# A two-layer retention and grouped-expert step on one core: states by row group inside the out-projection, squares summed by VectorE, root before reciprocal, logits by chunk with the router weights stationary

## The reference

```python
h = rms_norm(x, g_mix_norm[l]) * (1 + sc1) + sh1
mix, s_new, buf_new = token_mixers(h, ...)     # retention (4 heads of 128) and a 31-tap convolution
x = x + gt1 * (mix @ w_out[l])
h = rms_norm(x, g_ffn_norm[l]) * (1 + sc2) + sh2
ff = grouped_moe(h, w_router, b_router, w_exp_gate[l], w_exp_up[l], w_exp_down[l])
x = x + gt2 * ff
...
# retention, one step of a sampled sequence: the state that is returned
s = s * c_decay + einsum('bjhd,bjhe->bhde', kc * k_decay, vc)
# group norm of a head, and rms_norm: (o - mu) * lax.rsqrt(var + EPS)
# grouped_moe
probs = softmax(h @ w_router + b_router)       # 16 experts in 4 groups
g_sel = argmax(sum of the two best of each group)
wts, local = top_k(cand, 2); wts = wts / sum(wts)
counts = bincount(flat_e, length=16)           # rows of an expert, in blocks
(silu(xb @ w_gate[e]) * (xb @ w_up[e])) @ w_down[e]
```

## Time and profile before

| | before |
|---|---|
| median of 3 runs | 1499.33 us (1494.32 to 1500.7) |
| the profiled execution, its own time | 1502.44 us |
| its span | 1500.3 us |
| TensorE busy | 1428.7 us (95%) |
| VectorE busy | 682.3 us (45%) |
| ScalarE busy | 239.8 us (16%) |
| GpSimd busy | 104.6 us (7%) |
| mean granted TensorE clock | 0.974 |
| moved by DMA | 501.98 MB, 335 GB/s over the span |

### The profile page before, as it was taken

How to read it: one execution, slowest core, us unless ns; L and a number is a source line. 1 busy time by engine, 2 the same in 40 slices (tenths; PEclk the granted TensorE clock), 3 DMA queues, 4 the chain that set the end, 5 groups by cost and what they waited for, 6 DMA issues and landing times.

```text
span 1500.3 us, 19677 instructions
## 1 busy us (share of the span) xinstructions
PE 1428.7 (95%) x6993; PEld 658.7 (44%) x6994; DVE 682.3 (45%) x1986; ACT 239.8 (16%) x392; POOL 104.6 (7%) x149
## 2 busy tenths in 40 slices
PE   6999998999999999999989999999999999999996
PEld 2777664333333233333347766633333333333333
DVE  2697647333323333343338965553333323233333
ACT  1201322111111011111130122211111101111112
POOL 1071111000000000000002511100000000000000
PEclk9899998999999999999999999889999999999998
DMA  9944558999999985899998265589999999979991
GB/s 335 352 175 151 209 204 322 410 409 410 409 410 410 409 321 223 309 410 410 409 409 331 112 242 210 192 330 393 410 410 409 410 409 410 409 299 409 410 410 72
DMA packets 131317, 501.98 MB, mean 335 GB/s; under 512 B 8635, under 2 KB 8955, under 8 KB 131266
## 3 DMA queue, kind: packets, MB, share of 16 engines
q1 hardware_dynamic: 127056, 487.84, 82.5%
q0 software_dynamic: 3600, 11.21, 2.3%
q10 hardware_dynamic: 626, 2.46, 0.6%
HBM read 495.32 MB, written 7.00 MB: 335 GB/s over the span
## 4 chain that ended last, share of the span: by engine, by line
PE 60%; SPq 25%; DMA 5%; DVE 4%; issue 3%; ACT 2%; PEld 1%; PEldq 1%; ACTq 0%; DVEq 0%
PE ps L414 57%; SPq L380 18%; SPq L376 4%; PE ps L417 3%; DMA ring<-in_w_mod 2%; DMA ring<-in_w_exp_up 2%; SPq L396 1%; SPq L318 1%; PEld ps L414 1%; ACT hT L866 1%; ACT arena L866 1%; ACT L866 0%; SPq L382 0%; DVE stat L1053 0%; PEldq L563 0%
## 5 line engine op out<-in xcount | busy, mean ns | idle before, releaser
L414 PE MATMUL ps<-ring,arena 128*64 128x512 f32 x2816 | 635.7, 599 | 16.9 <-DMA ring<-in_w_exp_up 13.8
L414 PEld LDWEIGHTS ps<-ring,arena 128*64 128x64 f32 x2816 | 194.9, 137 | 404.7 <-issue 356.0
L866 ACT ACTIVATE arena<-ps 128x512 f32<-128x512 f32 (+3 forms) x240 | 129.6, 551 | 1124.8 <-PE ps L414 1033.9
L414 PE MATMUL ps<-arena 64*128 64x288 f32 (+4 forms) x1484 | 296.3, 505 | 12.0 <-DVE arena L1383 4.7
L414 PE MATMUL ps<-hT,ring 128*128 128x288 f32 x1024 | 257.9, 414 | 8.4 <-DVE hT L1127 4.1
L1416 DVE SCALAR_TENSOR_TENSOR xT<-ps,mod,xT 128x256 f32<-128x256 f32 x280 | 133.4, 476 | 267.7 <-PE ps L414 267.7
L414 PEld LDWEIGHTS ps<-hT,ring 128*128 128x128 f32 x1024 | 197.8, 194 | 66.4 <-issue 6.9
L414 PEld LDWEIGHTS ps<-arena 64*128 64x128 f32 (+4 forms) x1484 | 119.6, 161 | 203.0 <-issue 180.2
L1158 DVE SCALAR_TENSOR_TENSOR arena<-arena,wcT 128x256 f32<-128x256 f32 x240 | 123.5, 575 | 1.6
L1450 DVE TENSOR_TENSOR arena<-ps,arena 128x512 f32<-128x512 f32 x35 | 24.2, 692 | 195.9 <-PE ps L414 195.9
L417 PE MATMUL ps<-cst,arena 128*128 128x128 f32 (+5 forms) x533 | 83.0, 289 | 12.2 <-DVE arena L1040 7.2
(11 more groups left out here) (173 smaller groups left out, 628.3 us busy)
## 6 DMA issues: line engine op xcount, KB each, us to landing
ring<-in_w_exp_up SPq DMA_DIRECT2D x128, 1024.0 KB, 18.0
ring<-in_w_exp_down SPq DMA_DIRECT2D x128, 1024.0 KB, 17.7
ring<-in_w_exp_gate SPq DMA_DIRECT2D x64, 1024.0 KB, 17.8
ring<-in_w_mod SPq DMA_DIRECT2D x48, 1024.0 KB, 8.9
arena<-in_w_exp_gate SPq DMA_DIRECT2D x32, 1024.0 KB, 17.1
ring<-in_w_in SPq DMA_DIRECT2D x24, 1024.0 KB, 21.4
big<-in_w_exp_gate SPq DMA_DIRECT2D x16, 1024.0 KB, 18.2
hT<-in_w_exp_gate SPq DMA_DIRECT2D x16, 1024.0 KB, 18.4
```

Source lines behind the costliest of these rows:

```text
L414: return nc.tensor.matmul(out, lhsT, rhs, start=start, stop=stop, skip_group_check=True)
L866: return nc.scalar.activation(out, in_, f, **kw)
```

## The change

**Sampled states.** One GpSimd product makes the masked values of all four heads: head h stands in partitions 32h to 32h+31 (`vS` and `kdS` are laid out so by ScalarE copies and VectorE operations). `sample_states(g)` makes half the sequences of all four heads with four matmuls, one per group of 32 rows, each to a bank of its own. It runs inside the out-projection, after blocks 4 and 6, and VectorE adds the states there.

**Second norm.** VectorE adds the squares of chunks 1 to 6 onto that of chunk 0; TensorE sums two chunks instead of eight.

**Root first.** ScalarE takes the root straight from the bank, with the scaling and EPS in the same operation; VectorE takes the reciprocal after it. This holds for the first norm, the layer norm of the convolution, the four heads, the second norm and the last norm.

**Logits.** The router weights are stationary (16 columns), `hT` moves; for each chunk three matmuls write the three token tiles to three column groups. The logits come out expert by token; VectorE copies them, TensorE transposes them to token rows.

**Routing.** Softmax is not normalised; counts come by a matmul of their own, the comparison with block limits and the prefix sum by tables (`thr`, `below`) instead of chains; weights and some clearing are moved to other places.

```diff
+        kdS = kd[:, 2, 0:DH]
+        lgT = stat[:, 0, 0:P]
...
-                def head_states(i):
...
+                def sample_states(g):
+
+                    for h in range(H):
+                        hr = slice(h * NS, (h + 1) * NS)
+                        last = mm(ps[:, STATE_BANK[h], :], kdS[hr, :], vmask[hr, g * 512:(g + 1) * 512], True, True)
                     last.then_inc(V.snew_done, 1)
...
-                pe.wait_ge(V.var_ready, 3)
+                pe.wait_ge(V.rstd_ready, 3)
                 out_block(0, CONV_K)
...
                     out_block(m, RET_K).then_inc(V.outproj_done, 1)
+                    if m == 4:
+                        pe.wait_ge(V.vmask_ready, 1)
+                        pe.wait_ge(V.mod2_added, 3)
+                        sample_states(0)
+                    elif m == 6:
+                        pe.wait_ge(V.snew_ready, 1)
+                        sample_states(1)
...
-                feature_sum(7, sq2, KC, arrived=V.norm2_sq).then_inc(V.norm2_sum, 1)
-                pe.wait_ge(V.mod2_added, 3)
-                head_states(0)
-                head_states(1)
-
-                pe.wait_ge(V.x_mid, KC)
+                pe.wait_ge(V.norm2_acc, 1)
+                mm(ps[:, 7, 0:T], ones, sq2[:, 0, :], True, False)
+                pe.wait_ge(V.norm2_sq, KC)
+                mm(ps[:, 7, 0:T], ones, sq2[:, KC - 1, :], False, True).then_inc(V.norm2_sum, 1)
+                pe.wait_ge(V.x_mid, 7)
                 mod_slab(6, 1, layer_load(2))
                 pe.drain().then_inc(V.mod2_done, 1)
...
+                for k in range(KC):
+                    pe.wait_ge(V.h2_ready, k + 1)
+                    for t, (t0, m) in enumerate(TILES):
+                        last = mm(ps[32 * t:32 * t + E, 4, 0:m], wr[:, k, :], hT[:, k, t0:t0 + m], k == 0, k == KC - 1)
                 last.then_inc(V.logits_done, 1)
...
                         last.then_inc(V.h2_trans, 1)
                         n += 1
-
-                pe.wait_ge(V.h2_copied, 6)
-                head_states(2)
-                head_states(3)
+                        if n == 1:
+                            pe.wait_ge(V.lgT_ready, 1)
+                            tr(ps[:, 5, 0:96], lgT[0:96, :], 96).then_inc(V.lg_trans, 1)
...
-                mm(ps[:, 5, 0:4 * E], ones, mcum[:, :], True, False)
-                last = mm(ps[:, 5, 0:3 * E], C("tri"), rt[:, 10, :], False, True)
-                last.then_inc(V.pos_done, 1)
+                mm(ps[:, 5, 0:3 * E], C("tri"), rt[:, 10, :], True, False)
+                mm(ps[:, 5, E:3 * E], ones, mcum[:, 0:2 * E], False, True).then_inc(V.pos_done, 1)
+                pe.wait_ge(V.m_ready, 2)
+                mm(ps[:, 4, 0:E], ones, rt[:, 12, 0:E], True, True).then_inc(V.cnt_done, 1)
...
-            def root(buf):
-
-                a(buf, buf, ACT.Sqrt).then_inc(V.rstd_ready, 1)
+            def root(buf, bank, n):
+
+                a(buf, ps[:, bank, 0:T], ACT.Sqrt, scale=1.0 / n, bias=C("eps")).then_inc(V.rstd_ready, 1)
...
-                act.wait_ge(V.var_ready, 1)
-                root(stat[:, 1, :])
+                act.wait_ge(x_summed, l + 1)
+                root(stat[:, 1, :], 6, D)
...
+                        for h in range(H):
+                            last = a(vS[h * NS:(h + 1) * NS, :], ps[0:NS, 5, h * P:(h + 1) * P])
+                        last.then_inc(V.v_copied, 1)
...
-            def inverse_var(ch, dst, src, n):
-
-                ch.link(v.tensor_scalar(dst, src, 1.0 / n, EPS, ALU.mult, ALU.add))
-                v.reciprocal(dst, dst).then_inc(V.var_ready, 1)
...
+            def inverse(ch, buf, nth):
+
+                dve.wait_ge(V.rstd_ready, nth)
+                ch.link(v.reciprocal(buf, buf))
...
                 if l == 0:
-                    dve.wait_ge(x_summed, 1)
-                    inverse_var(ch, stat[:, 1, :], ps[:, 6, 0:T], D)
+                    inverse(ch, stat[:, 1, :], 1)
                 dve.wait_ge(slab_step, 4 * l + 2)
                 ch.link(add_turned(2, 1))
...
                 if l > 0:
-                    dve.wait_ge(x_summed, l + 1)
-                    inverse_var(ch, stat[:, 1, :], ps[:, 6, 0:T], D)
-                dve.wait_ge(V.rstd_ready, 1)
+                    inverse(ch, stat[:, 1, :], 1)
...
-                head_var(0)
-                head_var(1)
-                head_mix(0)
-                head_var(2)
-                head_mix(1)
-                head_var(3)
-                head_mix(2)
-                head_mix(3)
+                for h in range(H):
+                    head_mix(h)
...
+                for m in range(4, KC):
+                    add_gated(ch, lambda m: OUT_BANK[m % 4], M_GT1, V.outproj_done, V.x_mid, [m])
+                    if m == 4:
+                        for j in range(1, 4):
+                            ch.link(add_square(j))
+                        add_states(0)
+                    elif m == 6:
+                        ch.link(add_square(4))
+                        ch.link(add_square(5))
+                        add_square(6).then_inc(V.norm2_acc, 1)
+                        add_states(1)
...
+                for t, (t0, m) in enumerate(TILES):
+                    last = v.tensor_copy(lgT[32 * t:32 * t + E, 0:m], ps[32 * t:32 * t + E, 4, 0:m])
+                last.then_inc(V.lgT_ready, 1)
+                dve.wait_ge(V.lg_trans, 1)
...
-                ch.link(v.tensor_reduce(col(2), r3(1), AX.X, ALU.add))
-                ch.link(v.reciprocal(col(2), col(2)))
-                tt(r3(1), r3(1), over_e(col(2)), ALU.mult)
...
+                above = mixed[:, 0:E * (MAXSUB - 1)].rearrange("p (e s) -> p e s", e=E)
+                tt(above, bl(ps[:, 4, 0:E], MAXSUB - 1), C("thr").rearrange("p (e s) -> p e s", e=E), ALU.is_gt)
...
-            v.tensor_scalar(stat[:, 1, :], ps[:, 6, 0:T], 1.0 / D, EPS, ALU.mult, ALU.add).then_inc(fin_rs, 1)
+            dve.sem_inc(tick, 1)
...
-                for i, h in enumerate(STATE_ORDER):
-                    if i >= 2:
-                        pool.wait_ge(V.snew_done, i - 1)
...
-                for i, h in enumerate(STATE_ORDER):
-                    pool.wait_ge(V.snew_ready, i + 1)
-                    pool.dma_start(dstate(rets_v, h), state(h)).then_inc(V.states_stored if i < 2 else V.Sa_stored, 16)
+                gp.tensor_tensor(vmask.rearrange("p (b e) -> p b e", b=B), vS.unsqueeze(1).to_broadcast([P, B, DH]),
+                                 C("smask").unsqueeze(2).to_broadcast([P, B, DH]), ALU.mult).then_inc(V.vmask_ready, 1)
+                pool.wait_ge(V.snew_ready, 2)
+                for h in (2, 3, 0, 1):
+                    pool.dma_start(dstate(rets_v, h), state(h)).then_inc(V.states_stored if h >= 2 else V.Sa_stored, 16)
```

More of the change, by code:

```diff
@@ L68, in constants @@
     c["fold"] = fold.reshape(P, -1)
+    c["eps"] = np.full((P, 1), EPS)
     scale = DH ** -0.5
@@ L952, in _ @@
                 act.wait_ge(V.ln_scaled, 1)
-                act.wait_ge(V.ln_var, 1)
                 for ct in range(CT):
@@ new lines, in _ @@
+                v.tensor_tensor(mcum[:, E:2 * E], M[:, 0:E], M[:, E:2 * E], ALU.add).then_inc(V.m_ready, 1)
+                dve.wait_ge(V.m_ready, 1)
+                v.tensor_tensor(rt[:, 12, 0:E], mcum[:, E:2 * E], M[:, 2 * E:3 * E], ALU.add).then_inc(V.m_ready, 1)
+                pos = ps[:, 5, 0:3 * E].rearrange("p (t e) -> p t e", t=3)
+                dve.wait_ge(V.pos_done, 1)
+                ch.link(v.scalar_tensor_tensor(slot0, pos[:, :, 0], 1000.0, r3(10)[:, :, 0], ALU.add, ALU.mult))
@@ new lines, in _ @@
+                iota = C("iota")
+                for t in range(3):
+                    last = v.tensor_scalar(sel[:, t, :], iota[:, 0:BLK], 1000.0, slot0[:, t:t + 1], ALU.add, ALU.is_equal)
+                last.then_inc(V.sel0_ready, 1)
+                nsubs, starts = rt[:, 14, 0:E], rt[:, 14, E:2 * E]
+                dve.wait_ge(V.cnt_done, 1)
+                above = mixed[:, 0:E * (MAXSUB - 1)].rearrange("p (e s) -> p e s", e=E)
+                tt(above, bl(ps[:, 4, 0:E], MAXSUB - 1), C("thr").rearrange("p (e s) -> p e s", e=E), ALU.is_gt)
@@ new lines, in _ @@
+                ch.link(v.tensor_reduce(nsubs, above, AX.X, ALU.add))
+                v.tensor_scalar(nsubi[:, 0:E], nsubs, 1.0, None, ALU.add)
+                ch.link(v.tensor_scalar(nsubs, nsubs, 1.0, None, ALU.add))
+                ch.link(v.tensor_reduce(rt[:, 14, 2 * E:2 * E + 1], nsubs.unsqueeze(1), AX.X, ALU.add))
+                v.tensor_copy(nsubi[:, E:E + 1], rt[:, 14, 2 * E:2 * E + 1])
+                before = mixed[:, 0:E * E].rearrange("p (e s) -> p e s", e=E)
+                tt(before, bc(nsubs, E), C("below").rearrange("p (e s) -> p e s", e=E), ALU.mult)
@@ new lines, in _ @@
+                ch.link(v.tensor_reduce(starts, before, AX.X, ALU.add))
+                ch.link(v.scalar_tensor_tensor(r3(13), bc(starts, 3), float(BLK), pos, ALU.mult, ALU.add))
+                for k in range(2):
```

(29 more changed lines are left out.)

176 lines of the change are left out of this document (76 added, 100 removed).

## The result

| | before | after |
|---|---|---|
| median, measured side by side | 1496.84 us (4 runs) | 1478.43 us (4 runs, 1476.66 to 1481.89) |
| ratio after/before | | 0.9878 (95% interval 0.9845 to 0.991) |
| the profiled execution; its span | 1502.44; 1500.3 us | 1478.89; 1477.1 us |
| PE / DVE / ACT / POOL busy | 1428.7 / 682.3 / 239.8 / 104.6 us | 1396.5 / 674.9 / 241.5 / 93.1 us |
| mean granted TensorE clock | 0.974 | 0.982 |

What follows compares the result with a forecast made beforehand. Weight loads set the pace, with a chain of waits from last out-projection block to first expert block. Terms 3.2 + 2.0 - 13.45 - 9.65 - 0.5 - 1.7 = -20.1 took 1502.44 to 1482.3, the median to 1479.2; range 1470 to 1491.

Steps and rivals of the forecast that it cites:

- signs that were named: Trace marks for a right forecast, among them second layer's gather about 13 sooner and first odd gate 2.0 after first block.
- First norm: Norm before the in-projection: root first uncovers the reciprocal, +3.2 us in the first layer and +2.0 in the second.
- Heads: First out-projection matmul waits for ScalarE's root instead of VectorE's reciprocal of head 0: -1.1 us in each layer.
- TensorE keeps its clock: Rival: full clock kept in first out-projection matmuls (1.9 us) and gather (2.0), both layers: 7.8 less, 1471.4; chance 0.14.
- States: Sampled states placed inside the out-projection, on four row groups with nearly full overlap: +2.6 us per layer (2.1 to 8.5).
- that rival: The four row groups of the states' matmuls don't overlap: 11.7 us more, 1490.9; chance 0.12.
- no clock was lost in the out-projection: Rival: out-projection blocks 5 to 7 run at 1.2 GHz, 23.5 us, plus serial states 11.7: 1514.4, slower; chance 0.04.
- Sum of squares, root, scaling: Second norm, each layer: sum -3.0 us, root ready -0.65, `hT` scaled -2.0 without GpSimd's late masks; -5.65 together.
- Logits: Router logits end one matmul after the last chunk: -6.0 us second layer, -2.9 first; turning them costs +1.3 each.
- Positions, choice: Routing: softmax and choice -2.0 us per layer with nine fewer VectorE operations; positions -1.9 in the second layer, -1.2 first.
- Loads: Expert loop, first layer: earlier state stores let the odd gate issue sooner, as in the second layer: -1.7 us.
- the second rival: Weight loads hold the gain back: 1490.5 if the first layer's is lost, 1504.0 (no change) if both; chance 0.08.

Runs made afterwards that it cites:

- the two runs of after: The changed kernel, measured at 1478.43 us (ratio 0.9878), and the same kernel unaltered, run and profiled once more: 1479.41 us (ratio 0.9877).

## Why the prediction was right, and where it was not

The sum held stretch by stretch: what follows the norm is shorter since the squares, the states, the late mask and the old logits are out of the way. Put back one at a time, by the medians against the two runs of after, the states cost 6.8 to 7.7, the logits 4.5 to 5.5, the mask 2.7 to 3.7 and the squares 1 to 2. The shorter choice, positions and first selection, 9 in both layers, were not put back; they are read from the two profiles alone. Of the signs that were named, the second layer's gather starts 14.3 sooner behind the first out-projection matmul (forecast 13), and the first odd gates come 2.4 and 2.0 behind the first block.

*First norm.* +3.2 and +2.0, measured +3.3 and +2.1, returned when the old norm was put back. The cost was rightly found in the cover that the reciprocal lost.

*Heads.* The size was right, -0.9 and -1.0 for -1.1, the cause half so: the heads' roots alone are worth 0.6 to 0.7, the rest needs the layer norm's root as well, which I had not priced. The term was right in sum but left out a neighbour: the two together keep TensorE's clock, 1.7 more per layer. That is half of the rival "TensorE keeps its clock" (chance 0.14). Its other half, gather, did not happen in the first profile of after, and the run with unread products shows what it was worth: 1.3 in gather and 1.4 in the first block, where I had put 2.0.

*States.* +2.6, measured +2.5: twice 1.14 and 0.25 besides. The row groups overlap wholly: in after each pass of four starts within 0.02. So that rival is out, and no clock was lost in the out-projection. The 4.23 that the term started from was read too simply: the last of its eight instructions already ran at the half clock (1.06, where the others take 0.59 to 0.70). At the full clock all eight would take an estimated 3.8, so the four groups are 3.3 times as fast as one. The Trainium skill's drain at a change of tiling mode (TensorEngine Tiling (Array Packing), Tiling Modes, Key Properties) shows as at most those 0.25 for four changes, 0.06 each; the estimate from its latency formula was 0.17.

*Sum of squares, root, scaling.* -5.65, measured -5.7. Undoing single parts gives 2.87 and 1.65 where I had 3.0 and 2.0. But of the squares' 5.7 in both layers the time shows 1 to 2. The forecast added up lengths as though the clock behind them did not depend on them; that an idle TensorE runs gather and the first block more slowly would explain the difference, and isn't shown for the squares.

*Logits.* -6.0 and -2.9 with +1.3 came out within 0.1. I had explained the larger one by the states and the slab in front and by two token tiles behind the last chunk; the new logits alone bring 5 per layer up to the first gating, in part because the old ones, which had a clock of 0.98 in the earlier trace rows, run at 0.50 in this place.

*Positions, choice.* Within 0.3. *Loads.* -1.7, measured -1.7 in the first profile of after and -0.9 in the second, and in the first layer the stores were the cause; the second layer gave back 0.6 and 0.2. That blocks that start sooner wait longer for data would explain it. That the loads take a gain is the second rival in small; it bites in the first layer from an entry of about 36 down.

*Roots with a pointer operand.* They take 0.50 instead of 0.44. The root now reads PSUM as well, and a ScalarE operation of the same size that reads PSUM without a pointer takes 0.41:

```profile
57.83 0.41 ACT L872 ACTIVATE arena<-ps 128x288 f32<-128x288 f32 x1 [5.90 <-PE ps L419]
```

So the pointer costs 0.09, and the move to PSUM gives 0.03 back. The Trainium skill (ScalarE: Activation LUTs, What ACT_TABLE_LOAD costs) has 93 ns per pointer operand, and the trace agrees; the forecast's 0.8 for nine roots comes to 0.5, nine times 0.06.

The profiles differ by 23.6, where 20.1 was forecast: 2.5 in the in-projection against the change and 2.4 in the last norm for it vary from one execution to the next (1.7 and nothing beyond the forecast's 0.5 in the second profile of after), and the kept clock (-3.4) makes the rest. The medians differ by 18.4 only. The profiled execution of before lay 5.6 above the median of before (1496.84), that of after 0.5 above its own; which stretch of before was long in that execution one profile can't tell, and this stays open. So the time within 1 us of the forecast is a sum of errors of some 3 each way.

## What to carry to other kernels

Before an operation is reordered to shorten a chain, ask which wait covered it: root first won where VectorE's chain was the last to arrive and lost 5.5 where the reciprocal had run under a slab's copy. Work taken off TensorE while it waits can have a second price, the clock of what follows: feeding it unread products gained 5.2 here. And a stretch gained ahead of a weight stream counts only until the stream sets the end. When a part is put back by itself, read which wait replaces it: two of the runs here were decided by a wait that stood in neither theory (stores, and weights).

## What the runs showed of the hardware

Eight matmul instructions on four groups of 32 rows took 1.14 where the same on one group took 4.23, the last of them at half the clock. One GpSimd product of 2.07 made one VectorE operation of 0.47 last 2.12. The granted clock of identical code differs from one execution to the next by when it falls and rises: in kernels with the same code there the in-projection's first gate comes after 9.4 to 11.0, and the entry to the expert loop takes 35.6 to 39.1. Products with no reader kept TensorE at 2.4 GHz through gather in four of four cases and through the first block in three of four, at no cost that these profiles show. A ScalarE square root of 128x288 with a pointer bias took 0.50 from PSUM, a sigmoid of that size without a pointer 0.41.
